# Rotary products with the keys' low parts: one full-height product per 512 keys, or a pair of half-height products per 1024 keys

## The reference, cut to what matters

```python
q_rope = _rope(q_rope, cos[:, None, :], sin[:, None, :])
k_rope = _rope(k_rope, cos, sin)
...
s = (jnp.einsum('bqhd,bkhd->bhqk', qn, k_nope) + jnp.einsum('bqhd,bkd->bhqk', qr, k_rope)).astype(F32) * MLA_SCALE
p = jax.nn.softmax(s, axis=-1).astype(v.dtype)
return jnp.einsum('bhqk,bkhd->bqhd', p, v)
```

## Time and profile before

| | us |
|---|---|
| median of 3 runs | 3348.98 |
| lowest, highest | 3346.54, 3350.27 |
| the profiled execution | 3351.49 |
| its span from first to last instruction | 3349.9 |

### The profile page before, as it was taken

How to read it: one execution, slowest core, us unless ns; L and a number is a source line. 1 busy time by engine, 2 the same in 40 slices (tenths; PEclk the granted TensorE clock), 3 DMA queues, 4 the chain that set the end, 5 groups by cost and what they waited for, 6 DMA issues and landing times. The chain is left out here.

```text
span 3349.9 us, 44180 instructions
## 1 busy us (share of the span) xinstructions
PE 3254.7 (97%) x16472; PEld 2708.5 (81%) x16472; DVE 1666.9 (50%) x3113; ACT 1426.9 (43%) x2567; POOL 661.5 (20%) x458
## 2 busy tenths in 40 slices
PE   7999999999799999999999999999999999999999
PEld 6788888877588888788878888888888888887887
DVE  4899999836655565531223223232222523666311
ACT  5233232233466666520134535556445325664200
POOL 4212122122201111023221111011110212331231
PEclk9999999999899999999999999999999999999999
DMA  5333333367521111353333232232323344445521
GB/s 134 89 83 101 86 94 91 87 189 242 178 60 39 48 53 40 91 173 106 108 120 108 78 125 72 92 116 78 115 70 95 117 174 163 133 135 176 173 91 61
DMA packets 431620, 367.07 MB, mean 110 GB/s; under 512 B 76984, under 2 KB 367288, under 8 KB 431408
## 3 DMA queue, kind: packets, MB, share of 16 engines
q1 hardware_dynamic: 346400, 270.64, 28.0%
q10 hardware_dynamic: 85008, 93.61, 8.0%
HBM read 237.29 MB, written 126.86 MB: 109 GB/s over the span
## 5 line engine op out<-in xcount | busy, mean ns | idle before, releaser
L2787 ACT ACTIVATE eow_w1raw<-of_ring 128x512 f32<-128x512 f32 x218 | 126.7, 596 | 397.5 <-PE of_ring L3188 394.7
L879 PE MATMUL ef_ring<-ef_hhi,ef_whi 128*128 128x512 f32 x720 | 288.8, 401 | 1.9 <-issue 1.0
L881 PE MATMUL ef_ring<-ef_hhi,ef_wlo 128*128 128x512 f32 x720 | 281.3, 391 | 0.0
L880 PE MATMUL ef_ring<-ef_hlo,ef_whi 128*128 128x512 f32 x720 | 281.1, 390 | 0.0
L405 POOL TENSOR_TENSOR ef_wlo<-ef_wraw,ef_whi 128x1024 fp32r<-128x1024 f32 x29 | 86.1, 2970 | 482.4 <-ACT ef_whi L454 482.4
L3014 DVE SCALAR_TENSOR_TENSOR of_state<-of_state,of_small,of_tv 128x256 f32<-128x256 f32 x64 | 56.1, 877 | 242.0 <-ACT of_tv L2849 239.8
L879 PEld LDWEIGHTS ef_ring<-ef_hhi,ef_whi 128*128 128x128 f32 x720 | 135.5, 188 | 41.5 <-issue 14.7
L516 ACT ACTIVATE ef_stage<-ef_ring 128x512 f32<-128x512 f32 x90 | 53.5, 594 | 266.7 <-PE ef_ring L881 266.5
L881 PEld LDWEIGHTS ef_ring<-ef_hhi,ef_wlo 128*128 128x128 f32 x720 | 135.5, 188 | 29.3
L880 PEld LDWEIGHTS ef_ring<-ef_hlo,ef_whi 128*128 128x128 f32 x720 | 135.8, 189 | 26.1
L2704 POOL TENSOR_TENSOR eo_w0lo<-of_wraw,eo_w0hi 128x1024 fp32r<-128x1024 f32 x27 | 66.7, 2469 | 453.1 <-ACT eo_w0hi L2741 453.1
(11 more groups left out here) (663 smaller groups left out, 9403.0 us busy)
## 6 DMA issues: line engine op xcount, KB each, us to landing
of_wraw<-o_w_in SPq DMA_DIRECT2D x53, 512.0 KB, 3.9
ef_wraw<-e_w_in SPq DMA_DIRECT2D x29, 512.0 KB, 4.1
s_tmo<-eow_w1raw ACTq DMA_DIRECT2D x48, 256.0 KB, 2.3
ow_raw<-s_yt SPq DMA_DIRECT2D x18, 512.0 KB, 5.3
ow_raw<-o_w_out SPq DMA_DIRECT2D x16, 512.0 KB, 5.3
s_uc<-ef_stage ACTq DMA_DIRECT2D x24, 256.0 KB, 2.6
ef_ut<-s_uc SPq DMA_DIRECT2D x16, 384.0 KB, 4.1
s_za<-ef_stage ACTq DMA_DIRECT2D x24, 256.0 KB, 2.4
```

The source lines that it names most:

```text
L879: pe.matmul(out, ah, hhi[:, f, tc], start=(f == 0), stop=False)
L880: pe.matmul(out, ah, hlo[:, f, tc], start=False, stop=False)
L881: mm = pe.matmul(out, al, hhi[:, f, tc], start=False, stop=(f == KT - 1))
L2787: act.activation(stage[i % 4][:, :], ring[i % 3][:, :] if i else start.first, func, scale=GK ** -0.5 if name == "q" else 1.0).then_inc(eva ...
```

## The change

For tiles with two parts, L1846 is left out in both parts. In its place, after the other products of the second part, stand two products of 64 rows and 512 keys each. The first, in the upper half of the array's rows, multiplies `qr[0:64]` (the query's high part) by `krl[0:64]` of the first 512 keys and goes to the first bank; the second, in the lower half, multiplies `qrh[64:128]` (the high part again) by `krl[64:128]` of the second 512 keys and goes to the second bank. The low by low term is no longer computed there. Tiles with one part keep L1846. The number of matmuls stays ten per two-part tile.

`qrh` is a new tile with the query's high part in all 128 partitions. POOL now casts `qrr` into `qrh`, casts its upper 64 partitions once more into `qr`, and subtracts `qrh` instead of `qr`; `qr_hi` is raised twice per call, and SP's wait counts in fours. A new semaphore `half_done` is raised by the first product of the pair. DVE's `peak` waits for it in addition, and so does POOL before it overwrites `qr`. `gap2` is space that is not used.

```diff
+        s.sb("gap2", [P, 256])
+        qrh = s.sb("qrh", [P, T], F32R)
...
                     if h:
-                        sp.wait_ge(qr_hi, 2 * h)
+                        sp.wait_ge(qr_hi, 4 * h)
                         sp.wait_ge(qr_done, 2 * h)
...
                         pool.wait_ge(sc_done, 12 * h - (4 if long else 0))
-                    pool.tensor_copy(qr[:, t], qrr[:, t]).then_inc(qr_hi, 1)
-                    pool.wait_ge(qr_hi, 2 * h + (1 if long else 2))
-                    pool.tensor_tensor(qr[64:P, t], qrr[64:P, t], qr[64:P, t].bitcast(F32), ALU.subtract).then_inc(qr_done, 1)
+                        pool.wait_ge(half_done, 8 * h)
+                    pool.tensor_copy(qrh[:, t], qrr[:, t]).then_inc(qr_hi, 1)
+                    pool.wait_ge(qr_hi, 4 * h + (1 if long else 3))
+                    pool.tensor_copy(qr[0:64, t], qrr[0:64, t]).then_inc(qr_hi, 1)
+                    pool.wait_ge(qr_hi, 4 * h + (2 if long else 4))
+                    pool.tensor_tensor(qr[64:P, t], qrr[64:P, t], qrh[64:P, t].bitcast(F32), ALU.subtract).then_inc(qr_done, 1)
...
                     dve.wait_ge(sc_done, n + 1)
+                    if parts(n) == 2:
+                        dve.wait_ge(half_done, n // 12 * 8 + n % 12 + 1)
...
-                    mm = pe.matmul(out, qr[:, q], krl[:, k], start=False, stop=True)
-                    if c == parts(n) - 1:
-                        mm.then_inc(sc_done, 1)
+                    if parts(n) == 1:
+                        pe.matmul(out, qr[:, q], krl[:, k], start=False, stop=True).then_inc(sc_done, 1)
+                    elif c:
+                        first = slice(t0, t0 + 512)
+                        pe.matmul(sc[n % 2][:, cut(0)], qr[0:64, q], krl[0:64, first], start=False, stop=True).then_inc(half_done, 1)
+                        pe.matmul(out, qrh[64:P, q], krl[64:P, k], start=False, stop=True).then_inc(sc_done, 1)
```

More of the change, by code:

```diff
@@ L1352, in attention @@
         rope_out = [s.sem(f"rope_out{u}") for u in range(2)]
-        qr_in, qr_hi, qr_done = s.sem("qr_in"), s.sem("qr_hi"), s.sem("qr_done")
+        qr_in, qr_hi, qr_done, half_done = (s.sem(x) for x in ("qr_in", "qr_hi", "qr_done", "half_done"))
         sc_done, mx_done, nm_done, exp_done, rs_done, pr_done, tr_done, hi_done, lo_done, o_done, y_done = (
```

## The result

| | before | after |
|---|---|---|
| median of 20 runs each, us | 3348.71 | 3354.90 |
| lowest, highest | 3346.12, 3351.41 | 3352.68, 3358.82 |
| ratio to before, 95% interval | | 1.0019 (1.0013 to 1.0025) |
| span of the profiled execution | 3349.9 | 3353.2 |

The change costs 6.2 us (4.4 to 8.4 by the interval). The forecast was +7.7 us. In its terms the measured ratio, 1.0019, lies at the edge (0.2%) between "slower" and "the same". The interval lies wholly above 1, so the change does cost time, but it holds 1.002, so it does not tell on which side of that edge the loss falls.

The account below looks back on a forecast made before the run. TensorE's own sequence of products in attention was taken as the bound. Per tile 0.23 us won against 0.34 to 0.40 paid for tiling changes summed to +7.7: 3348.98 + 7.7 = 3356.7 us, range for 8 in 10 3352 to 3365.

Parts of the forecast that it names:

- The bound: In attention, TensorE's own sequence of products sets the time from about 930 us on; the other engines have slack.
- The removed products: Two L1846 products per two-part attention tile, 64 tiles x 2 x 0.23 us: 29.4 us of TensorE's time removed.
- Two streams at once: A pair of 64-row products in attention streams like one product, adding 64 x 0.23 = 14.7 us at best.
- The four edges: Gaps and weight loads entering and leaving the pair's half-row tiling: 0.32, 0.107, 0.313 us, and 0.165 for the first transpose step.
- The other edits: POOL's extra cast, the half_done and qr_hi waits and the shifted sc_done: each claimed to cost nothing under its cover.
- The sum: Attention tiles: 48 before transposes lose 0.11 us each, 14 before value products 0.165, the first 0.1; +7.7 us.
- the signs that the prediction named: Timeline after: 0.32 us into the pair, 0.31 out, no new TensorE wait, attention's last score product 7.7 us later.
- Rival 2: Entering and leaving the pair's row halves costs nothing; the change wins 14.2 us, 3334.8 us; chance 0.07.
- Rival 3: Leaving the pair's tiling costs nothing, one edge being hidden; -2 us in all, 3347 us; chance 0.09.
- Rival 1: The pair's two 512-column halves can't stream at full rate at once; +21.8 us in all, 3370.8 us; chance 0.10.
- rival 4: The pair's products run one after the other in the same half mode; same time as Rival 1, sharing its chance.
- The chances: For the whole kernel: slower 0.66, same 0.26, faster 0.08, with about 0.2% (6.7 us, 3355.7) as the line.

Follow-up runs that it names:

- e6_no_low: Changed kernel without L1846 or the pair for two-part tiles, low-part key products left out; 3320.5 us, 0.9916 of the kernel before.
- e5_one_of_pair: Changed kernel without the pair's upper product, the lower one kept with its half-row visit; 3356.3 us, 1.0016 of the kernel before.
- e4_two_visits: Changed kernel with the pair taken apart: upper product alone behind the first part, lower alone behind the second; 3392.8 us, 1.0131 of the kernel before.
- e1_full_rows: Changed kernel with only the tiling taken back, both products using all 128 rows; 3349.8 us, 0.9998 of the kernel before.
- e7_rows_96: As e4_two_visits, one product behind each part, but with 96 rows instead of 64; 3350.2 us, 1.0001 of the kernel before.
- e3_same_rows: Changed kernel with both products of the pair in the upper 64 rows; 3376.3 us, 1.0077 of the kernel before.

## Why the prediction was right, step by step

**The bound.** Right. e6_no_low won 0.232 us for every product taken out, and in none of the traces does TensorE wait for another engine between 932 and 1320 us.

**The removed products,** 128 x 0.23 = 29.4 us: 29.7 measured in e6_no_low.

**Two streams at once** for the price of one: right, now at 512 columns too, by e5_one_of_pair. I had kept 0.10 for the opposite, because the earlier trace rows show pairs only at half that rate; that was a fair reading of the rows, and it is closed now.

**The four edges.** The prediction took 0.32 into the pair, 0.107 for its load, 0.313 out of it and 0.165 for the first step of the transposes. After shows 0.32 in, 0.42 from the pair to the transposes (0.107 and 0.313 together; the rows do not part them), and transposes of 0.66 instead of 0.60. All four came from another stage with other shapes (192 columns, a split by columns for one of them, 32-column tiles for another), and the sums held. The transposes' load is the cheap 0.06, not the 0.107 of the upper bound. e4_two_visits measured the sum by itself, 0.346 us a visit; the prediction's terms give 0.32 + 0.107 + 0.313 + 0.165 less 0.23 + 0.23 + 0.11, which is 0.335, and 0.39 before value products, thus 0.34 in the mean of a head's 14 visits of the one kind and two of the other.

**The other edits cost nothing:** right, by e1_full_rows. Under its cover POOL's long split runs 1.1 us longer, and no one waits for it.

**The sum,** +7.7 us, against +7.2 by the length of a head and +6.2 in the medians. One small term was missing: with the second product moved from the first part to the end of the second one and no tiling changed, a head gets 0.09 us shorter (e1_full_rows), 0.7 us in all; why neighbouring full products run at 0.22 in one order and 0.24 in another stays open. Against e1_full_rows the tiling costs 0.98 us per head, 7.9 us in eight heads; the prediction's terms give 6 x 0.11 + 2 x 0.165 = 0.99 for a head. The 1.0 us between 7.2 and the medians is within their interval (4.4 to 8.4), and no run says where it comes from. One small figure of the prediction does not follow from its own numbers: 1.25 less seven times 0.162 and 0.107 leaves 0.009 between the two of a pair, not 0.007; after shows 0.01 at most, and nothing hangs on it.

Of the signs that the prediction named, one did not come out in the profiled executions: attention's last tile should start 7.7 us later and everything behind it too. It starts 5.4 us later (1391.63 before, 1397.04 after), and the whole span is 3.3 us longer. From tile 12 on attention grew by 6.3 us, as its steps say, but the first head took 62.37 us before and 61.30 after. Part of that is TensorE's clock where the pipeline of tiles fills. In the 14 us from 918 us on it was granted 0.77 of the full clock before and 0.88 after, each a mixture of the levels 1.2 and 2.4 GHz:

```profile
918.00:932.00 14.00, 10.47 (x36) 7.72 (x35) 7.55 (x13) 7.78 (x10) 0.00 (x0) 0.77 0.56 164
```

```profile
918.00:932.00 14.00, 10.98 (x44) 7.50 (x43) 8.68 (x14) 8.36 (x11) 0.00 (x0) 0.88 0.53 164
```

0.11 of 14 us is 1.5 us of full clock, and 44 matmuls against 36 went through. Two more such differences lie behind attention: in the 30 us from its last tile on the clock was 0.83 before and 0.89 after, and at 3060 to 3100 us 0.96 and 1.00. In all of these executions TensorE waits for ACT in the first of the three stretches. It is scatter between executions and doesn't come from the visits: two kernels have all the products and no visit at all, and of these e1_full_rows has 0.88 in that stretch and a first head of 61.26 us, and e7_rows_96, which comes to it 2.8 us later, has the 0.77 of before and 62.53 us:

```profile
921.00:935.00 14.00, 10.32 (x35) 7.58 (x34) 7.57 (x13) 7.75 (x10) 0.00 (x0) 0.77 0.54 164
```

So the difference of two profiled spans is not a measure of this change; the medians and the length of a head are.

**The rivals.** Rival 2, that the edges cost nothing here and the change is faster, is ruled out by e4_two_visits. The Trainium skill says ("TensorEngine Tiling (Array Packing)", Key Properties) that changing the tiling mode drains TensorE; the traces agree: 0.32 us into the half-row tiling where 0.23 is the pace, and 0.42 out of it. That the array empties in these gaps is not seen in a trace. e7_rows_96 adds that 96 rows pay nothing. Rival 3, one edge hidden, is out by the same rows, since both edges are there. Rival 1 is out by e5_one_of_pair, and rival 4, the two products one after the other, by their starts, 0.01 us apart; e3_same_rows shows what that would have cost.

**The chances.** 0.66 for slower by more than 0.2% and 0.26 for the same. The ratio is 1.0019, just under that line. The forecast had placed the sum one us above it, and the median came out 1.5 us lower: 0.5 us of that shows in the length of a head, the other 1.0 is not clear of noise. So on which side of the line the number fell was as much luck as forecast. The edge was known to be close; what would have helped is a look at how the pace varies between 0.22 and 0.24 in the earlier trace rows and its neighbours, since 0.01 us in a product is 0.6 us over 64 tiles.

## What to carry to other kernels

Running two half-height products at once is worth one stream (0.23 us at 512 columns), and going to the half-row tiling and back costs 0.35 to 0.39 us over one full product: a single pair between full products loses, two pairs in one visit win 0.10 us, so group them, and use the freedom of an accumulation's order to do so. To price such an edge, look in the trace of another stage for any place where the tiling changes, and read starts to starts, since busy time stays at 100% throughout. A product with 96 rows needed no such thought here; it ran at the pace of a full one (0.22 to 0.24 us).

## What the runs showed of the hardware that I had not expected

- A product of 96 rows pays no edge (0.22 us after L1852, 0.24 to the transposes), one of 64 rows in the same place pays 0.346 us per visit. Whether 65 to 95 rows behave as 96 wasn't tried.
- The first product in a new tiling is listed as starting with its own weight load: 0.49 us long instead of 0.39. A distance from it to the next product holds that load, which made my estimate for e3_same_rows read wrongly at first sight (0.33 from the first to the second, of which 0.107 is the load and 0.23 the stream). The parting into 0.107 and 0.23 is an estimate from the steps of the earlier trace rows and from the 0.24 us that a second stream adds.
- Two streams of 512 columns, in upper and lower rows and to two PSUM banks, cost each other nothing: a head of 61.68 us with both and 61.72 with one.
